# More seven-product double slots in the gate/up chunks of a hybrid decoder block, and the head's squares and sums in other slots

## What is computed

```python
def rmsnorm(x, g):
    y = xf * lax.rsqrt(jnp.mean(xf * xf, axis=-1, keepdims=True) + EPS)
    return (y * g.astype(jnp.float32)).astype(x.dtype)

def swiglu(h, wg, wu, wd):
    return (jax.nn.silu(h @ wg) * (h @ wu)) @ wd

x = x + 0.5 * swiglu(rmsnorm(x, ffn1_norm[i]), ffn1_wg[i], ffn1_wu[i], ffn1_wd[i])
x = x + hybrid_mixer(...)
x = x + 0.5 * swiglu(rmsnorm(x, ffn2_norm[i]), ffn2_wg[i], ffn2_wu[i], ffn2_wd[i])
return rmsnorm(x, final_norm)
```

## Time and profile before

| | |
|---|---|
| median of 3 runs | 1815.48 us (1813.77 to 1816.13) |
| profiled execution | 1814.53 us, of which the span is 1812.7 us |
| PE busy | 99% of the span, 8133 instructions |
| DVE busy | 86% |
| ACT busy | 57% |
| POOL busy | 14% |
| DMA | 367.28 MB moved, mean 203 GB/s |
| TensorE clock granted | full, in all of the 40 slices |

### The profile page before, as it was taken

One profiled execution on the slowest core, in us unless ns is written; L12 is line 12 of the kernel. 1 busy time (PEld: TensorE's weight loads), 2 busy tenths in 40 slices (PEclk: granted clock), 3 DMA queues, 4 the chain that ended last, 5 costly groups with the idle time before them and its releaser, 6 DMA issues.

```text
span 1812.7 us, 21956 instructions
## 1 busy us (share of the span) xinstructions
PE 1800.8 (99%) x8133; PEld 1483.0 (82%) x8134; DVE 1555.7 (86%) x1863; ACT 1024.2 (57%) x1334; POOL 245.1 (14%) x442
## 2 busy tenths in 40 slices
PE   9999999999999999999999999999999999999998
PEld 6888888888888888888788888888888888888886
DVE  7999998889999987678567867999999889999887
ACT  6555555455555556556577745555555455555554
POOL 1111111001111100000123300111111000221100
PEclk9999999999999999999999999999999999999999
DMA  7677776667677666766543655667676666677764
GB/s 240 212 209 215 216 217 213 197 200 216 211 217 212 211 201 213 210 205 201 151 130 115 209 174 181 208 210 218 207 217 213 212 206 194 209 219 223 242 202 149
DMA packets 199288, 367.28 MB, mean 203 GB/s; under 512 B 19012, under 2 KB 23856, under 8 KB 199056
## 3 DMA queue, kind: packets, MB, share of 16 engines
q1 hardware_dynamic: 185008, 352.37, 63.0%
q0 software_dynamic: 11648, 12.02, 2.2%
q10 hardware_dynamic: 2528, 1.52, 0.3%
HBM read 350.11 MB, written 4.19 MB: 195 GB/s over the span
## 4 chain that ended last, share of the span: by engine, by line
PE 98%; DVE 1%; ACT 1%; issue 0%; DMA 0%; ACTq 0%; DVEq 0%
PE ps L768 24%; PE ps L770 24%; PE ps L769 24%; PE ps L786 7%; PE ps L788 7%; PE ps L787 7%; PE ps L835 2%; DVE w_lo L1815 0%; PE ps L1066 0%; PE ps L1093 0%; PE ps L1068 0%; PE ps L1094 0%; PE ps L1196 0%; PE ps L1067 0%; PE ps L1166 0%
## 5 line engine op out<-in xcount | busy, mean ns | idle before, releaser
L1815 DVE TENSOR_TENSOR w_lo<-raw,w_hi 128x1024 fp32r<-128x1024 f32 x573 | 692.4, 1226 | 114.7 <-ACT w_hi L1302 110.9
L1302 ACT ACTIVATE w_hi<-raw 128x1024 fp32r<-128x1024 f32 x573 | 600.3, 1056 | 297.9 <-PE ps L770 212.2
L768 PE MATMUL ps<-w_hi,hT_hi 128*128 128x512 f32 x1308 | 512.6, 392 | 2.0 <-DVE w_lo L1815 1.1
L770 PE MATMUL ps<-w_hi,hT_lo 128*128 128x512 f32 x1308 | 509.6, 390 | 0.0
L769 PE MATMUL ps<-w_lo,hT_hi 128*128 128x512 f32 x1308 | 509.3, 389 | 0.0
L709 POOL DMA_DIRECT2D gu_raw<-gu_sq x352 | 187.1, 540 | 1078.5 <-DVE gu_sq L2061 1005.0
L1353 ACT ACTIVATE wt_hi<-wt 128x1024 fp32r<-128x1024 f32 x164 | 172.9, 1054 | 269.9 <-DVE wt L1877 269.9
L768 PEld LDWEIGHTS ps<-w_hi,hT_hi 128*128 128x128 f32 x1308 | 245.7, 188 | 53.4 <-DVE w_lo L1815 2.8
L770 PEld LDWEIGHTS ps<-w_hi,hT_lo 128*128 128x128 f32 x1308 | 245.5, 188 | 51.9
L769 PEld LDWEIGHTS ps<-w_lo,hT_hi 128*128 128x128 f32 x1308 | 245.7, 188 | 49.6
L1887 DVE TENSOR_TENSOR wt_lo<-wt,wt_hi 128x1024 fp32r<-128x1024 f32 x164 | 199.8, 1218 | 0.0
(11 more groups left out here) (306 smaller groups left out, 2222.1 us busy)
## 6 DMA issues: line engine op xcount, KB each, us to landing
raw<-in_ffn_wu_dram SPq DMA_DIRECT2D x176, 512.0 KB, 4.7
raw<-in_ffn_wd_dram SPq DMA_DIRECT2D x176, 512.0 KB, 4.8
raw<-in_ffn_wg_dram SPq DMA_DIRECT2D x175, 512.0 KB, 4.1
raw<-in_w_in_dram SPq DMA_DIRECT2D x88, 512.0 KB, 3.7
raw<-in_w_out_dram SPq DMA_DIRECT2D x32, 512.0 KB, 4.2
gu_raw<-gu_sq POOLq DMA_DIRECT2D x352, 32.0 KB, 3.6
x_parked<-x SPq DMA_DIRECT2D x8, 256.0 KB, 5.2
raw<-in_cmp_k_w_dram SPq DMA_DIRECT2D x8, 256.0 KB, 3.0
```

The lines of the kernel that those rows point to most:

```text
L768: mm(o, x_hi, w_hi[:, s, kk, :], start=begin, stop=False, skip_group_check=skip)
L770: ins = mm(o, x_lo, w_hi[:, s, kk, :], start=False, stop=last and kk == GK - 1, skip_group_check=skip)
L1302: act.activation(w_hi[:, c % SLOTS, :, :], raw[:, c % SLOTS, :, :], ACT.Copy).then_inc(hi_ready, 1)
L1815: tt(w_lo[:, s, :, :], raw[:, s, :, :], w_hi[:, s, :, :].bitcast(F32), ALU.subtract).then_inc(lo_ready, 1)
```

## The change

`THREE` gains the chunks 3, 7 and 9, so that all chunks from 2 to 10 have three double slots. `LATE` follows from it: in chunks 3, 7 and 9 the products are no longer summed at slots 14 and 15 but in slots 0 and 1 of the next chunk, and their own `gu_at` becomes 9 (the tenth slot) where it was 12.

The activation sums for the third pair (`h_sums(f, 1, ...)`) go from slot 14 of chunk 0 to slots 7 and 8 of chunk 1, `hs_high(f, 1)` from slot 15 of chunk 0 to slot 8 of chunk 1, `hs_low(f, 1)` from slot 8 to slot 9 of chunk 1. Their intermediate gets a place of its own (`h_late`, in the space of `hs_hi`).

In the head of the first part the four squares go from slots 1, 3, 5 and 6 to slots 7, 10, 11 and 14, the variance from slot 6 to 14, the root from 7 to 15 (ACT) and 7 to 15 (DVE), `hs_high(0, 0)` from 5 to 6, and DVE's `op[3]` from 6 to 7.

```diff
-THREE = (2, 4, 5, 6, 8, 10)
+THREE = (2, 3, 4, 5, 6, 7, 8, 9, 10)
...
+    late_at = at[0]
     hs_hi = sb("hs_hi", [P, 3, 4, P], F32R)
...
-    h_sum = sb("h_sum", [P, 3, CH])
+    h_sum = sb("h_sum", [P, 2, CH])
+    at[0] = late_at
+    h_late = sb("h_late", [P, 1, CH])
...
-                    after = {1: [sq[0]], 2: [op[1]], 3: [sq[1]], 4: [op[2]],
-                             5: [lambda: hs_high(0, 0), sq[2]], 6: [op[3], sq[3]], 7: [lambda: root(RS_FFN1)], 10: [vectors], 15: [lambda: hs_high(0, 1)]}
+                    after = {2: [op[1]], 4: [op[2]], 6: [lambda: hs_high(0, 0), op[3]], 7: [sq[0]],
+                             10: [vectors, sq[1]], 11: [sq[2]], 14: [sq[3]], 15: [lambda: root(RS_FFN1)]}
...
-                             5: [lambda: x_operand(2, NDC - 1)], 6: [lambda: root(RS_FFN2)], 15: [lambda: hs_high(1, 1)]}
+                             5: [lambda: x_operand(2, NDC - 1)], 6: [lambda: root(RS_FFN2)]}
...
+                        if n == 1 and p == 8:
+                            hs_high(f, 1)
...
-                             6: [op[3], lambda: hs_low(0, 0), lambda: variance(RS_FFN1, DM, NDC)],
-                             7: [lambda: inverse_root(RS_FFN1)]}
+                             6: [lambda: hs_low(0, 0)], 7: [op[3]], 14: [lambda: variance(RS_FFN1, DM, NDC)],
+                             15: [lambda: inverse_root(RS_FFN1)]}
...
-                after[14] = [lambda: h_sums(f, 1, 0), lambda: h_sums(f, 1, 1)]
...
-                            if n == 1 and p == 8:
+                            if n == 1 and p in (7, 8):
+                                h_sums(f, 1, p - 7)
+                            if n == 1 and p == 9:
                                 hs_low(f, 1)
```

More of the change, by code:

```diff
@@ L1908, in h_sums @@
                 no, k0, quads = 2 * f + late + 1, 2 if late else 4, 1 if late else 2
-                h = h_sum[:, sl, :].rearrange("p q (r t) -> p q r t", r=2)
+                h = (h_late if late else h_sum)[:, :, :].rearrange("p q (r t) -> p q r t", r=2)
                 block_ = lambda t, kk: h[:, :, kk, t * P:t * P + P]
```

## The result

The changed kernel takes 1818.11 us (median of 20 runs, 1815.43 to 1820.40), the kernel before 1814.82 us (20 runs, 1813.19 to 1816.13). The ratio is 1.0019, with a 95% interval of 1.0013 to 1.0026: slower by 3.3 us, 2.4 to 4.7. The forecast was +5.8 us. The sign is right, the size is not much over half of the forecast, and of the places where the matrix engine waits only a part was foreseen.

A forecast was written before the change was run, and what follows sets the result against it. The prediction took the matrix engine as the bound while DVE and ACT keep up. Matmuls -4.08, heads -1.1 and stalls +11.0 made +5.8 us, so 1815.48 became 1821.3 us, range 1811.0 to 1826.0.

The forecast's parts named there:

- (1): Chunks 3, 7 and 9 of both parts: one more pair each removes 18 matmuls, 4.08 us off the path.
- (2): Chunks 3, 7 and 9: a pair adds 4.3 us of DVE work, giving 41.7 us a chunk.
- lag: DVE's start of a chunk's up sums behind the matrix engine's start of that chunk; above 2.71 us the matrix engine stalls.
- (3): Late chunks with three pairs and gate sums: DVE waits for the second pair's load, taking 42.7 us a chunk.
- g: Growth of the lag per late chunk with three pairs and gate sums: 1.25 us, 42.7 against the matrix engine's 41.48.
- (4): Chunk 1: the activation sums delay DVE by 2.0 us, so the lag at chunk 2 is 1.8, not 0.20.
- (5): Starts of chunks 3, 4, 5 and 8, 9, 10: matrix engine stalls for the silu, 11.0 us in both parts.
- (6): Heads: moved squares and sums bring gate sums earlier, -1.0 us in the first part, -0.1 in the second.
- A: Second pair's loads in late chunks: the waits do not recur, g 0 to 0.3, -5.2 us; chance 0.17.
- B: Chunk 1: the activation sums are hidden, chunk 3 begins at lag 1.63, sum +3.0 us; chance 0.12.
- C: Late chunks: larger waits, g 1.43 to 1.83 as in early chunks, +8 to +12.8 us; chance 0.09.
- D: All chunks: DVE bounds every one, each added pair costs its 4.3 us, +26 us; chance 0.02.

The follow-up runs named there:

- half loads: The changed kernel with loads of gate/up chunks 1 to 10 bringing only the left half of each weight tile: 1808.11 us, ratio 0.9967.
- the moves alone: The changed kernel with the old `THREE`, so only the moved squares and sums are left: 1814.88 us, ratio 0.9999.
- the seven-chunk kernel: The kernel before with three pairs in chunks 2, 4, 5, 6, 7, 9 and 10: 1813.01 us, ratio 0.9992.
- the kernel before with the additions: The kernel before with one unused 128 x 512 DVE addition in each of chunks 2, 3, 4, 7, 8, 9: 1815.51 us, ratio 1.0005.
- early loads: The changed kernel with the low part of a pair's second slot made before those of the weight sums: 1813.23 us, ratio 0.9994.
- the pairs alone: The kernel before with only the new `THREE` (2 to 10), squares and sums where they were: 1820.34 us, ratio 1.0034.
- the changed kernel with additions: The changed kernel with one unused 128 x 512 DVE addition in each of chunks 2, 3, 4, 7, 8, 9: 1827.26 us.
- the run with the sums on POOL: The changed kernel with the gate sums and their low part made by POOL, not DVE: 1826.35 us, ratio 1.0062.
- the kernel before with early loads: The kernel before with the low part of a pair's second slot made before those of the weight sums: ratio 0.9999.

## Right and wrong, step by step

Of the waits of the matrix engine in the kernel before, the prediction counts three. Its view has two more, 1.2 us for the operand of the warm-up matmuls and 0.5 for the norm vectors' load, both in the first 5 us; the change touches neither.

**(1) Matmuls removed.** Right. 4.02 us come out when nothing else waits (half loads), 4.08 foreseen. The 216 ns that the prediction takes from the Trainium skill (TensorE: Matmul & The Clock Gate, Back-to-back issue gap) are there the gap of an isolated matmul; for a stream of matmuls of 512 columns the same section of the Trainium skill has about 131 ns. The streams here go at 227 ns, slower than either, and the measurement decides.

**(2) DVE's price of a pair.** Right: 41.3 us of work in the new chunks. It costs nothing by itself, since at growth 0.08 a chunk the lag stays below its limit.

**(3) The waits for loads, g.** Mis-sized. The twelve intervals in question had a mean of 42.45 (41.93 to 43.47), so g was 0.97 in place of 1.25, near the low edge of the forecast's own range for g (0.9 to 1.45) and above 0.76, where the sum changes its sign. DVE's waits for the load were 0.70 us in the mean. The row of chunk 5 showed the wait of a late chunk about right, at 0.61; on it I put 42.7 from the whole interval, which held two more waits, for ACT. DVE in order of time in the kernel before, chunk 5:

```profile
241.96 1.23 DVE L1815 TENSOR_TENSOR w_lo<-raw,w_hi 128x1024 fp32r<-128x1024 f32 x1 [0.25 <-ACT w_hi L1302]
...
249.51 1.22 DVE L1815 TENSOR_TENSOR w_lo<-raw,w_hi 128x1024 fp32r<-128x1024 f32 x1 [0.17 <-ACT w_hi L1302]
```

These 0.42 us do not come on top where a chunk has gate sums: ten of the twelve intervals have no wait of 0.1 us or more but the one for the load. That is most of the error of 0.28 in g: 0.42 less, against 0.09 more of wait for the load and the one wait of 0.85 for ACT, 0.07 in the mean. What chunk 5's row could not show is the spread: 0.30 to 1.79 us in equal chunks. The runs spread more too; they lay within 2.9 us before and within 5.0 after.

**(4) Activation sums in chunk 1.** Right: lag at chunk 2 of 1.74 and 1.75 (1.8 foreseen, 0.20 before), and DVE's wait for ACT in slot 9, 1.65 us:

```profile
77.36 1.23 DVE L1820 TENSOR_TENSOR w_lo<-raw,w_hi 128x1024 fp32r<-128x1024 f32 x1 [1.65 <-ACT w_hi L1305]
```

I had it costing only as a head start of the lag. With the old `THREE` it costs 0.6 us in the trace too, by the moves alone.

**(5) The lag and its limit.** The method held: the lag stops at 2.66 (2.71 foreseen), in both parts. By the measured numbers the sum is 12 x 0.97 = 11.6, less the 3.9 by which the lag may rise, 7.7 us, where 15 - 4.0 = 11.0 was foreseen. The place was wrong for most of it. I took the silu as the only limit; the first pair's low part has one of its own, some 0.3 lower, near 2.35. Three chunks show it that do not halt at their start: chunk 3 here, with a lag of 2.50, waits 0.15 there; chunk 10 of the seven-chunk kernel, with 2.44, waits 0.10; chunk 5 of the kernel before with the additions, with 2.47, waits 0.11. This limit catches PE again and again, also in the chunks 5 and 10, which I had at 41.48 and which took 41.94 to 41.98: 0.3 at the first pair, 0.1 in getting going after the halt at the start, the rest thinly spread. Four such chunks are 1.9 us, a term that the prediction put at nothing. 7.7 + 1.9 = 9.6, which is what was read from PE (9.65). So an error of -3.3 in size was partly covered by one of +1.9 in a thing unseen, which is luck. I had named "waits at another place, such as the pairs' low parts" as what would prove me wrong; in the place, it did.

**(6) The head.** Right: 48.12 for 49.13 us, -1.0. The wait for w_lo in the head, 1.1 before, is gone, and the gate sums of chunk 0 start at 51.74 and not at 54.26, one us earlier against the first matmul (43.79 after it and not 44.80). DVE in order of time, and the view of PE's waits, of the changed kernel:

```profile
51.74 0.69 DVE L1957 TENSOR_TENSOR ps<-ps,z 128x512 f32<-128x512 f32 x1
```

```profile
PE ps L771 <- ACT gu L1399: 1.2, 1, 1.2
```

The wait for the silu at chunk 1 is 1.2 where it was 0.7, since PE comes there 1.4 us sooner and the gate sums only 1.0. From those sums to the first matmul of chunk 1 it takes 4.33 us in both kernels (54.26 to 58.59 before, 51.74 to 56.07 after). ACT in order of time shows what fills them: a load of its table, then the silu, a high part between, and the second silu.

```profile
52.51 1.28 ACT L1399 ACT_TABLE_LOAD   x1 [1.75 <-DVE ps L1957]
...
55.34 0.68 ACT L1399 ACTIVATE gu<-ps,rs 128x512 f32<-128x512 f32 x1
```

The prediction's chain for the head had neither the table load nor the high part as something to gain; no run here moves them.

**Rivals.** A's mechanism exists (half loads, early loads), but needs loads that land in time. B, that the sums are hidden in chunk 1, is refuted by the lag of 1.74. Its time (+3.0) is nearer to the measured +3.3 than the forecast's, but by coincidence, as its mechanism is not there; its price of 1.4 a part (1.0 and 1.1 read) is no more than of the right order, given that equal stretches differ by 0.5 to 0.9. C asked for g of 1.43 and more; it was 0.97. D is refuted by the addition that costs nothing that can be told in the kernel before.

**What stays open.** The trace of one execution gives +4.0 us with the start taken out, the medians +3.3. The 6.2 us of the pairs alone and the -6.6 of the half loads are each over a microsecond more than their traces hold. And why a load takes 4.8 us in one chunk and 6.4 in the next was not tried. It is not all chance: the two longest of the twelve intervals are those from chunks 4 and 9 of the first part in the changed kernel (43.47, 43.02), in the pairs alone (43.28, 43.28) and in the changed kernel with additions (43.96, 44.29).

## What to carry to other kernels

Where one engine feeds another with little slack, follow its lag stage by stage, and take the limit at *each* place where the consumer waits, not at the one that the trace of before happens to show. Light stages between heavy ones are worth more than their busy share says: here they took back what a late load or an added instruction costs. And look at the operation that frees a buffer as well as at the one that makes the operand, since the two can compete for the same engine: the one 1.1 us earlier took the waits for loads away and brought waits of PE for the other.

## What the runs showed of the hardware

**Two engines on SBUF.** DVE's 128 x 1024 float32 subtraction takes 1.22 us alone and 1.48 beside POOL's additions and subtractions, 21% longer (the run with the sums on POOL).

**A halt costs more than itself.** After PE's waits for the silu or a low part in the changed kernel, the first matmul takes 0.33 us to the next start and not 0.227.

**The start.** The six warm-up matmuls ahead of the first product, in the profiled executions of the changed kernel and of the one before:

```profile
6.43 1.46 PE L896 MATMUL ps<-junk 128*128 128x512 bf16 x6
...
7.95 0.50 PE L880 MATMUL ps<-w_hi,hT_hi 128*128 128x512 f32 x1
```

```profile
6.85 2.56 PE L893 MATMUL ps<-junk 128*128 128x512 bf16 x6
```

The same six take 1.46 us in one (0.24 each) and 2.56 in the other (0.43 each), and the first product starts at 7.95 or 9.46. The seven warm-up matmuls at 1.19 us took 3.17 us in both (0.45 each), so in one execution PE had left that pace by the time of the six and in the other not. The view's granted clock reads 1.00 for all these stretches and does not tell them apart; what does was not tried. Over all fourteen profiled executions it started at 7.9 to 8.4 us in five and at 9.3 to 10.2 in nine, with kernels of either family in both groups: the kernel before with early loads had 8.04, the kernel before itself 9.46. Comparisons of two single executions carry this 1.5 us, which is nearly half of the change's 3.3.
